# Pairing the high and low rows in one 512-column matmul in four stages of a transformer kernel

## The reference, cut to what matters

```python
def swiglu(h, wi, wo):
    g, u = jnp.split(h @ wi, 2, axis=-1)
    return (jax.nn.silu(g) * u) @ wo

# second layer, x alone: ctx_out is False
x = x + g2 * o_l                                   # o_l = attention output @ w_o   (stage out_b)
x = ffn_step(x, sh3, sc3, g3, post_wi, post_wo)    # D_FF = 2816                    (stages wi3, wo3)
# hybrid layer
x = x + y                                          # y = mixed heads @ w_out        (stage out_c)
```

## Time and profile before

| what | value |
|---|---|
| median of 3 runs | 3002.62 us |
| the profiled execution's own time | 2999.55 us |
| its span in the profile | 2997.8 us |
| PE busy | 2844.3 us (95%), 16500 matmuls |
| PEld (weight loads, beside the matmuls) | 2381.9 us (79%) |
| DVE busy | 1692.1 us (56%) |
| ACT busy | 1229.5 us (41%) |
| POOL busy | 245.6 us (8%) |
| `out_b` | from about 1727 to 1756 us |
| `wi3` | from about 1762 to 1891 us |
| `wo3` | from about 1891 to 1955 us |
| `out_c` | from about 2099 to 2129 us |

### The profile page before, as it was taken

How to read it: one execution, slowest core, us unless ns; L and a number is a source line. 1 busy time by engine, 2 the same in 40 slices (tenths; PEclk the granted TensorE clock), 3 DMA queues, 4 the chain that set the end, 5 groups by cost and what they waited for, 6 DMA issues and landing times.

```text
span 2997.8 us, 47265 instructions
## 1 busy us (share of the span) xinstructions
PE 2844.3 (95%) x16500; PEld 2381.9 (79%) x16500; DVE 1692.1 (56%) x2909; ACT 1229.5 (41%) x1986; POOL 245.6 (8%) x163
## 2 busy tenths in 40 slices
PE   7999999997999999999998889997899999999999
PEld 4777886753878888888885489995898999888888
DVE  3333348766533334433348465586589777677765
ACT  4322234255322223322234454456445455445444
POOL 2000013200100001000011000000068100000000
PEclk9999999998999999999999999999999999999999
DMA  7444232262152232322323445551466555677764
GB/s 272 169 168 168 99 99 71 78 243 88 37 197 96 98 101 90 105 98 93 105 97 119 163 153 181 195 189 48 141 201 195 171 173 172 199 241 240 243 202 141
DMA packets 144845, 445.09 MB, mean 148 GB/s; under 512 B 16088, under 2 KB 44888, under 8 KB 144224
## 3 DMA queue, kind: packets, MB, share of 16 engines
q1 hardware_dynamic: 112896, 409.51, 40.7%
q10 hardware_dynamic: 31840, 34.13, 3.2%
HBM read 428.37 MB, written 15.20 MB: 148 GB/s over the span
## 4 chain that ended last, share of the span: by engine, by line
PE 82%; DVE 10%; ACT 3%; DMA 2%; issue 1%; SPq 1%; POOL 0%; ACTq 0%; DVEq 0%
PE bank L1759 20%; PE bank L1761 20%; PE bank L1760 20%; PE bank L2213 12%; PE bank L1775 2%; PE bank L2185 2%; PE bank L2036 1%; DVE w_lo L1111 1%; ACT w_hi L629 1%; PE bank L2077 1%; DMA raw<-w_stream_dram 1%; PE bank L1782 1%; PE bank L2048 1%; DVE cand L1544 1%; PE bank L2068 1%
## 5 line engine op out<-in xcount | busy, mean ns | idle before, releaser
L1759 PE MATMUL bank<-H,w_hi 128*128 128x256 f32 (+1 forms) x3344 | 1110.3, 332 | 28.3 <-DVE H L1144 11.6
L1111 DVE TENSOR_TENSOR w_lo<-raw,w_hi 128x1024 fp32r<-128x1024 f32 x584 | 714.8, 1225 | 657.5 <-ACT w_hi L629 652.2
L1761 PE MATMUL bank<-H,w_lo 128*128 128x256 f32 (+1 forms) x3344 | 1082.7, 324 | 0.0
L1760 PE MATMUL bank<-H,w_hi 128*128 128x256 f32 (+1 forms) x3344 | 1082.6, 324 | 0.0
L629 ACT ACTIVATE w_hi<-raw 128x1024 fp32r<-128x1024 f32 x628 | 660.0, 1052 | 224.5 <-PE bank L1761 175.3
L1759 PEld LDWEIGHTS bank<-H,w_hi 128*128 128x128 f32 x3344 | 641.5, 192 | 115.7 <-issue 47.9
L1760 PEld LDWEIGHTS bank<-H,w_hi 128*128 128x128 f32 x3344 | 641.5, 192 | 53.2 <-issue 4.9
L1761 PEld LDWEIGHTS bank<-H,w_lo 128*128 128x128 f32 x3344 | 640.7, 192 | 49.9
L1759 PE MATMUL bank<-act_hi,w_hi 128*128 128x512 f32 (+1 forms) x770 | 267.4, 347 | 0.0
L1761 PE MATMUL bank<-act_hi,w_lo 128*128 128x512 f32 (+1 forms) x770 | 266.9, 347 | 0.0
L1760 PE MATMUL bank<-act_lo,w_hi 128*128 128x512 f32 (+1 forms) x770 | 266.9, 347 | 0.0
(11 more groups left out here) (225 smaller groups left out, 2762.4 us busy)
## 6 DMA issues: line engine op xcount, KB each, us to landing
raw<-w_stream_dram SPq DMA_DIRECT2D x704, 512.0 KB, 3.3
ada_side<-w_stream_dram SPq DMA_DIRECT2D x52, 512.0 KB, 3.7
gelu_scratch<-gelu ACTq DMA_DIRECT2D x108, 128.0 KB, 3.5
gelu_in<-gelu_scratch ACTq DMA_DIRECT2D x108, 128.0 KB, 3.4
ada_start<-w_stream_dram SPq DMA_DIRECT2D x16, 512.0 KB, 13.7
bias<-bias_in_dram ACTq DMA_DIRECT2D x1, 3072.0 KB
X<-x_in_dram SPq DMA_DIRECT2D x1, 2048.0 KB, 10.3
mem<-mem_in_dram SPq DMA_DIRECT2D x1, 1024.0 KB, 16.9
```

The lines of the kernel that those rows point to most:

```text
L1111: nc.vector.tensor_tensor(w_lo[:, s, :], raw[:, s, :], w_hi[:, s, :].bitcast(F32), ALU.subtract).then_inc(lo_ready, 1)
L1759: nc.tensor.matmul(to, w_hi[:, s, cut], hi, start=first, stop=False, skip_group_check=True)
L1760: nc.tensor.matmul(to, w_hi[:, s, cut], lo, start=False, stop=False, skip_group_check=True)
L1761: return nc.tensor.matmul(to, w_lo[:, s, cut], hi, start=False, stop=last, skip_group_check=True)
```

## The change

In the four stages, `w_hi` multiplies the high and the low rows in one matmul of 512 columns. The columns of the high part end in the left half of a bank, those of the low part in the right half, and `w_lo` times the high part (256 columns) goes to the left half as well. So a step of k has two matmuls in place of three, and a bank's two halves have yet to be added. For that `act_hi` and `act_lo` become the two halves of one buffer `act`. In `wi3` VectorE adds the halves of each bank with a `tensor_reduce` over pairs of columns 256 apart: the gate to `stage_z`, from which ScalarE then takes silu, the up product to `stage_sq`. In the three stages that add to X, VectorE makes two updates of a row, one from each half, the second waiting for the first. The last row of each of these three stages (m = 7) stays as it was.

```diff
-        act_hi = sb("act_hi", [P, FC, 2 * NT], arena, F32R)
-        act_lo = sb("act_lo", [P, FC, 2 * NT], arena + 44 * KB, F32R)
+        act = sb("act", [P, 2, FC, 2 * NT], arena, F32R)
+        act_hi, act_lo = act[:, 0], act[:, 1]
...
+        def halves_of(buf):
+            return buf.rearrange("p (a n) -> p n a", a=2)
...
+        def paired(u, m):
+            return UPDATES[u][0] == "L" and m < KC - 1
...
-                        act.wait_ge(tile_used, t + 1 + 4 * i)
-                        nc.scalar.activation(stage_raw[:, jj, 0:w], bank[2 * jj][:, 0:w], ACT.Silu
-                                             ).then_inc(silu_done, 1)
+                        gate = bank[2 * jj][:, 0:w]
+                        if halves == "L":
+                            act.wait_ge(gate_added, 2 * i + jj + 1)
+                            gate = stage_z[:, jj, 0:NT]
+                        else:
+                            act.wait_ge(tile_used, t + 1 + 4 * i)
+                        nc.scalar.activation(stage_raw[:, jj, 0:w], gate, ACT.Silu).then_inc(silu_done, 1)
...
+                        if paired(u, m):
+                            link(update(m, 0, bank[4 + m % 4][:, 0:NT], gate(m, 0)))
+                            ins = update(m, 0, bank[4 + m % 4][:, NT:2 * NT], gate(m, 0))
...
                         split(t + AHEAD, i, 4)
+                        if halves == "L":
+                            dve.wait_ge(tile_used, t + 1 + 4 * i)
+                            nc.vector.tensor_reduce(stage_z[:, jj, 0:NT], halves_of(bank[2 * jj][:, :]), AX_X, ALU.add
+                                                    ).then_inc(gate_added, 1)
                         split(t + 1 + AHEAD, i, 4)
+                        dve.wait_ge(tile_used, t + 2 + 4 * i)
+                        up_of = bank[2 * jj + 1][:, 0:w]
+                        if halves == "L":
+                            up_of = stage_sq[:, jj, 0:NT]
+                            ins = nc.vector.tensor_reduce(up_of, halves_of(bank[2 * jj + 1][:, :]), AX_X, ALU.add)
+                            ins.then_inc(up_added, 1)
+                            dve.wait_ge(up_added, 2 * i + jj + 1)
                         dve.wait_ge(silu_done, j + 1)
-                        dve.wait_ge(tile_used, t + 2 + 4 * i)
-                        nc.vector.tensor_tensor(stage_y[:, jj, 0:w], stage_raw[:, jj, 0:w], bank[2 * jj + 1][:, 0:w],
-                                                ALU.mult).then_inc(a_ready, 1)
+                        nc.vector.tensor_tensor(stage_y[:, jj, 0:w], stage_raw[:, jj, 0:w], up_of, ALU.mult
+                                                ).then_inc(a_ready, 1)
...
+            def paired_passes(to, s, block_at, both, hi, first, last):
+                cut = slice(block_at * P, (block_at + 1) * P)
+                nc.tensor.matmul(to[:, :], w_hi[:, s, cut], both, start=first, stop=False, skip_group_check=True)
+                return nc.tensor.matmul(to[:, 0:NT], w_lo[:, s, cut], hi, start=False, stop=last, skip_group_check=True)
```

More of the change, by code:

```diff
@@ L266, in program @@
         a_ready = sem("a_ready")
+        gate_added = sem("gate_added")
+        up_added = sem("up_added")
         act_hi_ready = sem("act_hi_ready")
@@ L1249, in rows_out @@
                         dve.wait_ge(tile_used, RING[stage] + per * (m + 1))
-                        for half in range(len(halves)):
-                            ins = update(m, half, bank[4 + m % 4][:, half * NT:(half + 1) * NT], gate(m, half))
+                        if paired(u, m):
+                            link(update(m, 0, bank[4 + m % 4][:, 0:NT], gate(m, 0)))
+                            ins = update(m, 0, bank[4 + m % 4][:, NT:2 * NT], gate(m, 0))
+                        else:
+                            for half in range(len(halves)):
+                                ins = update(m, half, bank[4 + m % 4][:, half * NT:(half + 1) * NT], gate(m, half))
                         ins.then_inc(x_done, 1)
@@ L1761, in passes, with paired_product @@
                 return nc.tensor.matmul(to, w_lo[:, s, cut], hi, start=False, stop=last, skip_group_check=True)
+            def paired_passes(to, s, block_at, both, hi, first, last):
+                cut = slice(block_at * P, (block_at + 1) * P)
+                nc.tensor.matmul(to[:, :], w_hi[:, s, cut], both, start=first, stop=False, skip_group_check=True)
+                return nc.tensor.matmul(to[:, 0:NT], w_lo[:, s, cut], hi, start=False, stop=last, skip_group_check=True)
+            def paired_product(to, t, i=0, per=0):
+                pe.wait_ge(lo_ready, split_at(t) + 1 + per * i)
+                for k in range(KC):
+                    ins = paired_passes(to, t % R, k, H[:, 0, :, k, :], h_ap(0, k, "L"), k == 0, k == KC - 1)
+                ins.then_inc(tile_used, 1)
             def product(to, t, halves, i=0, per=0):
@@ L1878, in first_by_halves, with first_products @@
                         x_sums(n["update"], "C")
-            def first_products(name, targets, t0, halves):
+            def first_products(name, targets, t0, halves, paired_stage=False):
                 if NORMS[name]["by_halves"]:
@@ L1896, in first_products @@
                     for n, to in enumerate(targets):
-                        ins = passes(to[:, 0:w], (t0 + n) % R, k, h_ap(0, k, halves), h_ap(1, k, halves), k == 0,
-                                     k == KC - 1)
+                        if paired_stage:
+                            ins = paired_passes(to, (t0 + n) % R, k, H[:, 0, :, k, :], h_ap(0, k, "L"), k == 0,
+                                                k == KC - 1)
+                        else:
+                            ins = passes(to[:, 0:w], (t0 + n) % R, k, h_ap(0, k, halves), h_ap(1, k, halves), k == 0,
+                                         k == KC - 1)
                         if k == KC - 1:
@@ L1904, in ffn, with wi_product @@
                 t0, t1 = RING[f"wi{f}"], RING[f"wo{f}"]
+                def wi_product(to, t, i=0, per=0):
+                    if halves == "L":
+                        paired_product(to, t, i, per)
+                    else:
+                        product(to, t, halves, i, per)
                 def steps(i, side, done):
                     if isinstance(i, int) and i == 0:
-                        first_products(name, bank[0:AHEAD], t0, halves)
+                        first_products(name, bank[0:AHEAD], t0, halves, halves == "L")
                         if f == 0:
@@ L1915, in steps @@
                             side_product(f, 0, 0)
-                        product(bank[AHEAD], t0 + AHEAD, halves)
+                        wi_product(bank[AHEAD], t0 + AHEAD)
                         if side:
@@ L1920, in steps @@
                     for q in range(4):
-                        product(bank[q], t0 + q, halves, i, 4)
+                        wi_product(bank[q], t0 + q, i, 4)
                         if q == 0 and done:
@@ L1943, in row @@
                             j = KC * kk + k
-                            ins = passes(to[:, cut], t % R, k, act_hi[:, j, cut], act_lo[:, j, cut], j == 0, j == FC - 1)
+                            if paired(update, m):
+                                ins = paired_passes(to, t % R, k, act[:, :, j, 0:NT], act_hi[:, j, 0:NT], j == 0, j == FC - 1)
+                            else:
+                                ins = passes(to[:, cut], t % R, k, act_hi[:, j, cut], act_lo[:, j, cut], j == 0, j == FC - 1)
                             if j == sums_at:
@@ L2100, in project_out @@
                 if name:
-                    first_products(name, bank[4:4 + AHEAD], t0, halves)
+                    first_products(name, bank[4:4 + AHEAD], t0, halves, halves == "L")
                 def row(m, half, sums_at=None):
@@ L2107, in row @@
                     whole_row = m < KC - late(update)
+                    if paired(update, m):
+                        paired_product(bank[4 + m % 4], t0 + m)
+                        return
                     if whole_row:
```

## The result

The changed kernel takes 3042.47 us (median of 4 runs, 3037.73 to 3045.93), the kernel before, on the same chip, 3003.11 us (4 runs, 2999.59 to 3009.61). The ratio is 1.0128, 95% interval 1.0105 to 1.0150: 39.4 us slower. The forecast was 3040 us and 37.9 us slower. The profiled execution has a span of 3041.0 us.

What follows compares the result with a forecast made beforehand. The prediction took `wi3` to become bound by ScalarE and VectorE hand-overs, TensorE waiting. Its terms, 3.6 + 30.7 + 3.6 = 37.9 us, gave 3037.5 us against the profiled execution and 3040 us as median, range 3023 to 3062.

Steps and rivals of the forecast that it cites:

- Who sets the pace now: Before the change, TensorE bounds `wi3` and `wo3`, splits and updates bound `out_b` and `out_c`; `wi3` has 1.5 us cover per pair.
- TensorE's gain: All four stages: a step of k falls from 0.358 to 0.3445 us, 13.5 ns less, 8.3 us over 618 steps if exposed.
- `out_b` and `out_c`: A second update adds 0.52 us a row to the 3.39 us chain, 3.6 us slower in each stage.
- `wi3`: Reduces join the ScalarE and VectorE chain; a pair takes 7.15 us, TensorE needs 5.51; first high part 2.68 us later.
- The two loop extras: `wi3` loop: 0.56 rather than 0.45 us from multiply to high part, plus 0.05 to silu, making 6.99 into 7.15 us.
- `wo3`: Its first row waits for `wi3`'s late low part and a split, 32.5 us delay; later rows win 1.8, leaving 30.7 us.
- the low clock: Rival: gaps in `wi3` drop TensorE to 1.2 GHz for good, a pair costs 10.2 us, total 3108 us; chance 0.02.
- The sum: Whole kernel: 3.6 + 30.7 + 3.6 = 37.9 us slower, 3037.5 us profiled, 3040 us as a median.
- The reduce by values written: Rival: a reduce in `wi3` takes 0.42 us rather than 0.686, 12 us less, 3028 us; chance 0.06.
- the reduce at half pace: Rival: values 1 KB apart slow each `wi3` reduce by 0.53 us, 23 us more, 3063 us; chance 0.05.
- The covered adds: Rival: a `wi3` pair stays under 5.51 us; 2994 us if updates hide too (0.03), 3003 if they pay (0.04).

Runs made afterwards that it cites:

- e4: Changed kernel, but in `wi3` ScalarE makes both splits of a pair before silu and the next pair's first split before this pair's high part; 3006.59 us, ratio 1.0004.
- e6: e4's kernel, but in `out_b` and `out_c` ScalarE also splits the next row's tile ahead of this row's squares; 2982.33 us, ratio 0.9939 to the kernel before.
- e7: Kernel before, unpaired, with only ScalarE's split of the next row's tile moved ahead of the squares in `out_b` and `out_c`; 2996.30 us, ratio 0.9969.
- e8: The kernel of e4 run once more, unchanged, to see TensorE's pace; one execution, 2999.58 us.
- e9: The kernel of e6 run once more, unchanged, to see TensorE's pace; one execution, 2991.30 us.

## Why the prediction was right

Its steps in order.

**Who sets the pace now** was the step that decided. A view of busy shares says that DVE and ACT had half of `wi3` free, and by it 1.37 us more in a pair would fit. The pair of 7.21 us shows that view to be wrong for this order. e4 shows the same work to fit under another one: in `wi3` the place was the matter, not the amount.

**TensorE's gain.** Taken as 13.5 ns a step, and measured as 13.3. The 0.1193 and 0.2252 us of the prediction come from counts in 50 us, and such a count takes in matmuls that had started before the window. From start to start the trace of before has 0.1200 us (153 steps of three in `wo3`, 1898.65 to 1953.73, 0.3600 each) and 0.2267 us (1450.21 to 1499.85, 219 distances). So both were some 0.6% too low, and the difference came out nearly right. The changed kernel's step is 0.3467 us, the sum of the two, both in `out_b` (47 steps) and in `wo3` (131 steps, 1940.92 to 1986.34). At the other pace, 0.3533, the gain is 6.7 ns, which the prediction didn't know of. The Trainium skill (TensorE: Matmul & The Clock Gate, section Back-to-back issue gap) gives the rule of columns / 2.4 ns plus 2.5 ns for an isolated matmul and says itself that a stream goes by other figures. No run here has an isolated one, so these traces don't test the rule, as the prediction took them to do.

**`out_b` and `out_c`** were said to lose 3.6 us each and lost 3.64 and 3.52. The row's period came to 3.91, as the sum of 3.39 and 0.52.

**`wi3`.** First high part 2.68 us later relative to the stage: (1785.05 - 1766.09) - (1774.18 - 1757.89) = 2.67. Period 6.99 written out: 6.97 (1785.05 to 1792.02). In the loop 7.15, measured 7.21. The two loop extras were put in the wrong place: the hand-over from the gate's reduce to silu has none (0.72), the one from the up reduce to the multiply has 0.09, and every second pair pays 0.08 at the loop's edge. Over 20 pairs that is 1.2 us.

**`wo3`.** One detail failed. At the third tile TensorE was to run its six steps in 2.07 us and then wait 1.2 us for the fourth tile's split. It ran them in 3.50 us, from 1937.42 to 1940.92, and didn't wait:

```profile
1938.20 0.63 PE L1796 MATMUL bank<-act,w_hi 128*128 128x512 f32 x1
1938.62 0.41 PE L1797 MATMUL bank<-act,w_lo 128*128 128x256 f32 x1
1938.84 0.63 PE L1796 MATMUL bank<-act,w_hi 128*128 128x512 f32 x1
```

The steps stand 0.64 us apart, at a granted clock of 0.53 (1937.5 to 1940.5), the lower level (1.2 GHz), after 2.60 us of idle. The prediction had the low clock as a rival for `wi3`, and not here. The fourth tile began at 1940.92, where the prediction's terms, with the measured pairs, put 1940.56. That the low clock cost only 0.36 us is luck: the forecast wait would have stood in its place.

**The sum.** 30.7 us for `wi3` and `wo3` against 32.3: 1.2 from the period and 0.36 from the low clock. The steps that carry the sum held. The forecast of 3040 is 2.5 us low, of which 1.6 is this sum and the rest lies within the scatter of the medians.

**The rivals.** The reduce by values written and the reduce at half pace fall by the 682 and 684 ns. The clock stayed at 1.00 in `wi3`, with gaps of 0.2 to 0.9 us at the waits. The covered adds came true only where the order was changed (e4 to e6), and in `out_c` not even there.

## What to carry to other kernels

Before work is moved to an engine that looks half idle, write down its queue order and that of its partner, and follow one round of the hand-overs; the time that this takes, against the bound's, says what may be added. Add up as well what that engine does in a round, for when the chain is cut this is the next bound, as in e6's `out_c`. When an added instruction goes into such a chain, look for a neighbour in the partner's queue that needs none of it, and put that first. A gain on the bound engine is real only while it stays the bound: here 3 to 7 us were to be had from TensorE, 39 were paid, and, by the stages, 11 lay in the order of the queues without any change to the matmuls. And a pace is read from the distance of starts, not from a count in a window.

## What the runs showed of the hardware

- Two updates of 0.48 us with a same-engine wait between them start 0.52 us apart (1739.29 and 1739.81 in e6), and the pair takes 1.00 us. A split that didn't wait for the update ahead of it started 0.40 us after it (2113.66 and 2114.06 in e7).
- A `TENSOR_REDUCE` of 512 values of a bank takes 682 to 686 ns whether they are neighbours, 1 KB apart or one value twice.
- At a granted clock of 1.00 a stream of fp32r passes starts one each 0.1200 us with 256 columns and each 0.2267 us with 512. The second 256 columns cost 106.7 ns, so each pass has a part of 13.3 ns that doesn't go by columns, and this is what a pair saves.
- In a mixed stream of 512 and 256 columns a step has one of two paces, 0.3467 or 0.3533 us, at an unchanged granted clock, which moved `wi3` and `wo3` by 3.21 us. The all-512 stretch (1450 to 1500 us) has 0.2267 us in both e8 and e9.
- After TensorE's idle time of 2.78 us at the start of the changed `out_b`, the paired passes stand 0.43 and 0.21 us apart at a granted clock of 0.52 (1732 to 1735), the lower level (1.2 GHz), and a step costs 0.64 us. Three passes of 0.21 cost the same: pairing wins nothing there.
